# One stage for the three stream branches, with keys laid out by the host

## The reference

```
h = x @ W_in, split into queries, keys, values and gates of three branches
a: causal attention, 8 heads of 64, logit += F[t] - F[s], F = cumsum(log sigmoid(forget gate))
b: window of 128 cached keys (2 key heads for 8 query heads) + own chunk, with a sink per head
c: latent attention: keys and values are projections of a cached latent of 256, + rotary key of 32
branch_n = W_n( attention_n * silu(gate_n) );  m = sum_n sigmoid(g_n) * branch_n
x <- LayerNorm(alpha * x + m @ W_o)
```

## Time and profile before

| | us |
|---|---|
| median of three runs | 3997.64 |
| profiled execution | 3992.19 |
| its span | 3990.5 |
| stream stages of the first layer, a, b, c | 103.0, 43.7, 102.0 |
| stream stages of the second layer | 248.3 |

### The profile page before, as it was taken

One profiled execution on the slowest core, in us unless ns is written; L12 is line 12 of the kernel. 1 busy time (PEld: TensorE's weight loads), 2 busy tenths in 40 slices (PEclk: granted clock), 3 DMA queues, 4 the chain that ended last, 5 costly groups with the idle time before them and its releaser, 6 DMA issues. The chain is left out here.

```text
span 3990.5 us, 57004 instructions
## 1 busy us (share of the span) xinstructions
PE 3496.3 (88%) x21478; PEld 2913.6 (73%) x21478; DVE 1494.3 (37%) x3500; ACT 937.2 (23%) x2080; POOL 122.9 (3%) x64
## 2 busy tenths in 40 slices
PE   1999978998989986789869999789989899758988
PEld 0888856887978864568758888478889788545777
DVE  5114333343333324344531233333333333332546
ACT  1221212332223322220121112123322233212210
POOL 0000000000100000000000000001010000000000
PEclk9999988999999988889979999889999899879999
DMA  5322234223332234353442221433143322433543
GB/s 184 109 94 90 65 116 125 55 65 83 97 85 70 62 93 148 110 192 133 143 152 91 90 88 56 151 87 79 35 109 80 93 61 63 140 125 106 203 148 106
DMA packets 480642, 416.98 MB, mean 104 GB/s; under 512 B 301268, under 2 KB 392020, under 8 KB 478100
## 3 DMA queue, kind: packets, MB, share of 16 engines
q1 hardware_dynamic: 451172, 373.97, 31.1%
q10 hardware_dynamic: 29296, 40.71, 3.0%
HBM read 289.32 MB, written 127.64 MB: 104 GB/s over the span
## 5 line engine op out<-in xcount | busy, mean ns | idle before, releaser
L353 PE MATMUL proj_acc<-proj_wh,keep_xh 128*128 128x512 f32 (+1 forms) x1296 | 502.3, 388 | 12.4 <-DVE proj_wl L328 12.4
L354 PE MATMUL proj_acc<-proj_wl,keep_xh 128*128 128x512 f32 (+1 forms) x1296 | 501.0, 387 | 0.0
L355 PE MATMUL proj_acc<-proj_wh,keep_xl 128*128 128x512 f32 (+1 forms) x1296 | 500.9, 387 | 0.0
L353 PEld LDWEIGHTS proj_acc<-proj_wh,keep_xh 128*128 128x128 f32 x1296 | 244.6, 189 | 58.8 <-DVE proj_wl L328 13.2
L354 PEld LDWEIGHTS proj_acc<-proj_wl,keep_xh 128*128 128x128 f32 x1296 | 244.6, 189 | 45.5
L355 PEld LDWEIGHTS proj_acc<-proj_wh,keep_xl 128*128 128x128 f32 x1296 | 244.5, 189 | 45.5
L1918 PE MATMUL up_acc<-up_wh,up_bh 128*128 128x512 f32 x432 | 173.4, 401 | 12.8 <-DVE up_wl L1962 12.8
L328 DVE TENSOR_TENSOR proj_wl<-proj_raw,proj_wh 128x512 fp32r<-128x512 f32 (+1 forms) x144 | 96.0, 674 | 209.5 <-ACT proj_wh L323 209.5
L1058 PE MATMUL att_b_gacc<-att_b_gwh,keep_xh 128*128 (+1 forms) x576 | 171.0, 297 | 3.6 <-DVE att_b_gwl L1187 3.6
L1058 PE MATMUL att_c_gacc<-att_c_gwh,keep_xh 128*128 (+1 forms) x576 | 170.8, 297 | 3.2 <-DVE att_c_gwl L1187 3.2
L1058 PE MATMUL att_a_gacc<-att_a_gwh,keep_xh 128*128 (+1 forms) x576 | 170.0, 295 | 1.9 <-DVE att_a_gwl L1187 1.9
(11 more groups left out here) (357 smaller groups left out, 7147.1 us busy)
## 6 DMA issues: line engine op xcount, KB each, us to landing
up_gates<-scratch_gates SPq DMA_DIRECT2D x18, 1536.0 KB, 7.6
proj_raw<-in_w_in SPq DMA_DIRECT2D x48, 512.0 KB, 3.7
str_a_kc<-in_cache_a_k SPq DMA_DIRECT2D x16, 1024.0 KB, 5.5
str_a_vc<-in_cache_a_v SPq DMA_DIRECT2D x16, 1024.0 KB, 7.5
scratch_sg<-proj_out SPq DMA_DIRECT2D x54, 256.0 KB, 2.1
up_br<-scratch_br SPq DMA_DIRECT2D x54, 256.0 KB, 8.1
scratch_gates<-att_a_gout SPq DMA_DIRECT2D x24, 384.0 KB, 2.6
scratch_gates<-att_b_gout SPq DMA_DIRECT2D x24, 384.0 KB, 2.7
```

The source lines that it names most:

```text
L353: nc.tensor.matmul(bank, hi, wh[:, u, kt, 0:w], start=kt == 0, stop=False)
L354: nc.tensor.matmul(bank, hi, wl[:, u, kt, 0:w], start=False, stop=False)
L355: mm = nc.tensor.matmul(bank, lo, wh[:, u, kt, 0:w], start=False, stop=kt == KT - 1)
```

## The change

One stage takes the place of the three. Its eight rounds handle streams 0 to 7, each with all three branches, and its loops are written out.

- The host lays out the cached keys of a and b, the rotary keys of c and the key weights of c with positions (or ranks) last. Key tiles of a and b are used as they land, so are c's rotary keys; c's latents are still transposed, since they serve as values too.
- Own columns are 16 per stream: keys are sliced out of one transposed tile, values are loaded per stream to 16 partitions, the own masks of 128 columns are gone. A mask of 16 columns is left for a, in bf16, loaded once at the program's start.
- All streams' query columns are laid out once, in the head; the per-stream copies are gone. The forgetting term is split in a high and a low part in fp32r, so that one pass adds it. b's sink is written to its score column once.
- a and b are not scaled before the turn: the reciprocal and the gate are applied at the copy-out of their values. Their gates are loaded in the layout of the scores, by 8 loads each, issued by ScalarE at the end of its head, and the results are stored by 8 stores each. c is scaled as before.
- Score tiles are single per branch, the probabilities too; the three branches share one output bank, and two transpose banks with fixed readers (ScalarE for one, VectorE for the other).
- SyncE issues a stream's loads in the order keys of a, values of a, c, each behind the wait for its buffer; the early weights come behind the last stream's.

```diff
+        "c_mask_o": neg(np.arange(TS)[None, :] <= qt[:, None]),
...
@@ stream_attention: SyncE @@
+            def load_a(n):
+                u = n % U
+                if n >= U:
+                    sp.wait_ge(sa_made, n - U + 1)
+                sp.dma_start(ka[:, u], T["cache_a_kT"].rearrange("l b (g p) s -> l b p g s", p=P)[l, n])\
+                    .then_inc(a_loaded[u], 16)
+            def load_va(n):
+                u = n % U
+                if n >= U:
+                    sp.wait_ge(pva_made, n - U + 1)
+                sp.dma_start(va[:, u], T["cache_a_v"].rearrange("l b (t p) h d -> l b p t (h d)", p=P)[l, n])\
+                    .then_inc(va_loaded[u], 16)
+                sp.dma_start(voa[:, u], T["s_a_v"].rearrange("l b s h d -> l b s (h d)")[l, n])\
+                    .then_inc(va_loaded[u], 16)
+            def load_c(n):
+                u = n % UC
+                if n >= UC:
+                    sp.wait_ge(pvc_made, n - UC + 1)
+                sp.dma_start(kc[:, u], T["cache_c_kv"].rearrange("l b (t p) r -> l b p t r", p=P)[l, n])\
+                    .then_inc(c_loaded[u], 16)
+                sp.dma_start(pct[:, u], T["cache_c_peT"][l, n]).then_inc(c_loaded[u], 16)
+                sp.dma_start(voc[:, u], T["s_c_kv"][l, n]).then_inc(c_loaded[u], 16)
+            load_a(0)
...
+            for n in range(1, NB):
+                load_a(n)
+                load_va(n)
+                load_c(n)
+            sp.dma_start(C["early"][:], w_br_tiles(T, l)[:, 0:EARLY, :]).then_inc(early_loaded, 16)
+            def place(name, tile, h, wanted):
+                sp.dma_start(S[name][own].rearrange("(n t) (h d) -> h t n d", t=TS, h=H)[h],
+                             tile[h * TS:(h + 1) * TS, :, wanted]).then_inc(stored, 16)
+            sp.wait_ge(oa_taken, NB)
+            for h in range(H):
+                place("br0", oma, h, slice((h % 2) * HD, (h % 2) * HD + HD))
+            sp.wait_ge(ob_taken, NB)
+            for h in range(H):
+                place("br1", omb, h, slice(0, HD))
+            sp.wait_ge(res_ready, 1)
+            sp.dma_start(S["br2"][own], res[:]).then_inc(stored, 16)
+            sp.wait_ge(early_loaded, 16)
+            sp.wait_ge(stored, 16 * (2 * H + 1))
...
@@ TensorE, after the head @@
+            def keys_c(n):
+                u = n % UC
+                pe.wait_ge(c_loaded[u], 48 * (n // UC + 1))
+                for k, (bank, made, taken, group) in enumerate(((tr0, tr0_made, tr0_taken, G0["keys", n]),
+                                                                (tr1, tr1_made, tr1_taken, G1["keys", n]))):
+                    if group > 1:
+                        pe.wait_ge(taken, group - 1)
+                    for j in range(KB):
+                        mm = nc.tensor.transpose(bank[:, j * P:(j + 1) * P], kc[:, u, j, k * P:(k + 1) * P], ident)
+                    mm.then_inc(made, 1)
+            def scores_a(n):
+                u = n % U
+                pe.wait_ge(a_loaded[u], 16 * (n // U + 1))
+                if n >= 1:
+                    pe.wait_ge(exp_a, n)
+                cols = slice(n * TS, (n + 1) * TS)
+                for lo, w, keys in ((0, NK, ka[:, u]), (NK, TS, ktoa[:, :, cols])):
+                    for g in range(4):
+                        nc.tensor.matmul(ssa[32 * g:32 * g + 32, lo:lo + w], qxa[:, n, g, :], keys[:, g, :],
+                                         start=True, stop=False, skip_group_check=True, tile_position=(0, 32 * g))
+                nc.tensor.matmul(ssa[:, 0:NK], selr[:, n, :], fsplit[:, 0:NK], start=False, stop=True,
+                                 skip_group_check=True)
+                nc.tensor.matmul(ssa[:, NK:NK + TS], selr[:, n, :], fsplit[:, NK + n * TS:NK + (n + 1) * TS],
+                                 start=False, stop=False, skip_group_check=True)
+                nc.tensor.matmul(ssa[:, NK:NK + TS], C["ident16"][:], C["mask_o"][:], start=False, stop=True,
+                                 skip_group_check=True).then_inc(sa_made, 1)
+            def scores_b(n):
+                if n == 0:
+                    pe.wait_ge(b_loaded, 48)
+                else:
+                    pe.wait_ge(exp_b, n)
+                nc.tensor.matmul(ssb[:, 0:P], qxb[:, n, :], kb[:, n, :], start=True, stop=True)
+                nc.tensor.matmul(ssb[:, P:P + TS], qxb[:, n, :], ktob[:, n * TS:(n + 1) * TS], start=False, stop=True,
+                                 skip_group_check=True).then_inc(sb_made, 1)
+            def scores_c(n):
+                u = n % UC
+                pe.wait_ge(tr0_taken, G0["keys", n])
+                pe.wait_ge(tr1_taken, G1["keys", n])
+                if n >= 1:
+                    pe.wait_ge(exp_c, n)
+                cols = slice(n * TS, (n + 1) * TS)
+                for lo, w, keys, pes in ((0, NK, ktc[:], pct[:, u]), (NK, TS, ktoc[:, :, cols], kpoc[:, cols])):
                     for k in range(2):
+                        nc.tensor.matmul(ssc[:, lo:lo + w], qac[:, k, n, :], keys[:, k, :], start=k == 0, stop=False)
+                    mm = nc.tensor.matmul(ssc[:, lo:lo + w], qpt[:, n, :], pes, start=False, stop=True)
+                mm.then_inc(sc_made, 1)
...
+            def values_b(n):
+                pe.wait_ge(tr1_taken, G1["b", n])
+                pe.wait_ge(oa_taken, n + 1)
+                for k in range(KVB):
+                    half = slice(k * HD, (k + 1) * HD)
+                    nc.tensor.matmul(oo[half, 0:HD], ptb[:, half], vb[:, n, half], start=True, stop=False,
+                                     skip_group_check=True, tile_position=(0, k * HD))
+                for k in range(KVB):
+                    half = slice(k * HD, (k + 1) * HD)
+                    mm = nc.tensor.matmul(oo[half, 0:HD], pob[:, half], vob[:, n, half], start=False, stop=True,
+                                          skip_group_check=True, tile_position=(0, k * HD))
+                mm.then_inc(pvb_made, 1)
+            def values_c(n):
+                u = n % UC
+                pe.wait_ge(tr0_taken, G0["c", n])
+                pe.wait_ge(tr1_taken, G1["c", n])
+                pe.wait_ge(ob_taken, n + 1)
+                for k in range(2):
+                    for j in range(KB):
+                        nc.tensor.matmul(oo[:, k * P:(k + 1) * P], kc[:, u, j, k * P:(k + 1) * P], ptc[:, j, :],
+                                         start=j == 0, stop=False)
+                    mm = nc.tensor.matmul(oo[:, k * P:(k + 1) * P], voc[:, u, k * P:(k + 1) * P], poc_t[:],
+                                          start=False, stop=True)
+                mm.then_inc(pvc_made, 1)
+            for n in range(NB):
+                keys_c(n)
+                scores_a(n)
+                if n >= 1:
+                    turn_c(n - 1)
+                    values_b(n - 1)
+                scores_b(n)
+                if n >= 1:
+                    values_c(n - 1)
+                turn_a(n)
+                scores_c(n)
+                turn_b(n)
+                values_a(n)
+            turn_c(NB - 1)
+            values_b(NB - 1)
+            values_c(NB - 1)
+            pe.wait_ge(oc_taken, NB)
...
@@ ScalarE, end of its head and the rounds @@
+            for r, sem in ((0, gate_ab), (1, gate_ab)):
                 for h in range(H):
+                    name, tile, cols = (("sg0", sga, slice(h // 2 * P, h // 2 * P + P)),
+                                        ("sg1", sgb, slice(h * HD, (h + 1) * HD)))[r]
+                    const(sem, tile[h * TS:(h + 1) * TS],
+                          S[name][own].rearrange("(n t) c -> t n c", t=TS)[:, :, cols])
+            const(gate_c, sgc[:], S["sg2"][own])
...
+                take(taken, ktc[:, 0, :])
+                if n >= 1:
+                    taken += 1
+                    take(taken, ptc[:].rearrange("p j n -> p (j n)"))
+                exps(ssa, pa, NK + TS, sta, n, max_a, exp_a)
+                exps(ssb, pb, P + TS + 1, stb, n, max_b, exp_b)
+                taken += 1
+                take(taken, pta[:].rearrange("p j n -> p (j n)"))
+                exps(ssc, pc, NK + TS, stc, n, max_c, exp_c)
...
@@ VectorE, the rounds @@
+                nc.vector.tensor_copy(ktc[:, 1, :], tr1[:]).then_inc(tr1_taken, 1)
+                highest(ssa, NK + TS, sta, n, sa_made, max_a)
+                if n >= 1:
+                    taken += 1
+                    take_own(taken, poc_t[:])
+                    if n == 1:
+                        dve.wait_ge(gate_ab, 32 * H)
+                    out_b(n - 1)
+                highest(ssb, P + TS + 1, stb, n, sb_made, max_b)
+                if n >= 1:
+                    out_c(n - 1)
+                taken += 1
+                take_own(taken, poa[:])
+                highest(ssc, NK + TS, stc, n, sc_made, max_c)
+                taken += 1
+                dve.wait_ge(tr1_made, taken)
+                nc.vector.tensor_copy(pob[:], tr1[0:TS, P:2 * P])
```

(57 more changed lines are left out.)

793 lines of the change are left out of this document (271 added, 522 removed).

## The result

The changed kernel takes 3807.9 us (median of 4 runs, 3804.8 to 3809.8) against 3998.9 before: ratio 0.952, 95% interval 0.951 to 0.954. That is 191 us saved where 215 were forecast; the time lies 25 us above the forecast of 3783.

What follows compares the result with a forecast made beforehand. TensorE was taken to bound the rounds, mostly waiting in three heads and tails. Per layer 28.9 + 16 + 82.6 + 13.5 = 141.0 against 248.6 and 248.3, saving 214.9: 3783 us, range 3757 to 3850.

Steps and rivals of the forecast that it cites:

- One stage, one head, one tail; rounds bound by TensorE: Stream stages: one per layer replaces three, 141.0 us against 248.6 and 248.3, TensorE over 95% busy in rounds; chance 0.66.
- hand-offs (14.5): Rival, steady rounds: single banks and tiles stretch a round by 1.28 to 14.5 us, total 3821; chance 0.25.
- half the clock: Rival, all rounds: gaps keep TensorE at 1.2 GHz, +11.3 us a round, total 3961; chance 0.04.
- slow loads: Rival, loads through SyncE in order: under 101 GB/s a round exceeds 27.1 us; at 90 GB/s total 4043; chance 0.02.
- The round, 11.8: Steady round of the merged stage: TensorE's steps plus waits take 11.8 us, bounds 11.1 to 12.6.
- sum of 11.3: TensorE's steps in one round, priced by start-to-start times in the earlier trace, add to 11.3 us before waits.
- 0.4 for b's copy-out: Round: values c waits for values b's copy-out from the shared output bank, 0.4 us, between 0 and 1.0.
- Kept as they are: c's values: Round: c's value passes keep their earlier price, 2 x 1.12 = 2.24 us.
- Own pairs of c at 0.14: Scores of c: three own pairs of 16 columns at 0.14 us each, from a one-column pair, 0.42 together.
- fp32r passes 0.23 apart: Scores of a, forgetting term: one fp32r pass of 512 columns, 0.23 us, replaces a two-pass fp32 matmul of 1.06.
- The first round, 16, behind 17 issues: First round: 17 small gate loads issued by ScalarE take 8.8 us and delay TensorE; 16 us, bounds 9.3 to 21.
- Head 28.9, tail 13.5: Each layer's stage: 28.9 us before the rounds, bounds 24.3 to 43.8, and 13.5 us after them.

Runs made afterwards that it cites:

- pad_pe: Changed kernel with the position part of c's scores (32 rows of weights and keys) zero-filled to 128 rows, own values left at 16 rows: 3800.1 us, ratio 0.950.
- all: Changed kernel with own values of a, b, c and c's position part zero-filled to 128 rows, and gate loads moved off ScalarE's path: 3775.1 us, ratio 0.944.
- best: On top of `all`: scores a ahead of c's key transposes, b's first scores wait for keys alone, second stream's keys loaded before b's values: 3790.3 us, ratio 0.948.
- reorder: Changed kernel with only the order of c's value passes changed, the four 16-row passes together after all 128-row ones: 3798.4 us, ratio 0.950.

## Why the prediction was off by 25 us

- *One stage, one head, one tail; rounds bound by TensorE*: right. TensorE is busy for 13.27 of 13.27 us; the rivals of hand-offs (14.5), of half the clock and of slow loads did not come about. The loads cost nothing in steady rounds, at 207 GB/s.
- *The round, 11.8*: wrong by 1.48, and this is the failed step. Its sum of 11.3 measured 13.27 with hardly a wait (of the 0.4 for b's copy-out about 0.1 is left: scores b's two own passes take 0.30, two such passes of c 0.20 in `pad_pe`). By terms, forecast to measured: values c 2.24 to 2.97, scores c 3.28 to 3.74, scores b 0.36 to 0.62, keys c 0.87 to 1.02, turns 1.30 to 1.58, values a 1.23 to 1.36, values b 0.40 to 0.53, scores a 1.64 to 1.45.
- *"Kept as they are: c's values"*: not kept. The own keys' part shrank from 128 rows to 16, which I did not price. Padding it back took 0.99 off the round: two thirds of the miss.
- *What is left*: with the rows padded in `all` the round is 11.70, still 0.4 above the sum of 11.3. Keys c (1.03 for 0.87), the turns (1.54 for 1.30) and scores b (0.61 for 0.36) are dearer than forecast, the scores of a and c cheaper. The dear ones stand beside tiles of 32 and 64 columns, and there, too, the load does not run ahead: in the changed kernel c's first key transpose behind a's values and its load both start at 1557.10. `best` took one such place out, for 0.11; that the others cost the same was not tried.
- *Own pairs of c at 0.14*: 0.29, the six passes 0.87 where I had 0.42. I took the row of a lone pair between wide passes and set the Trainium skill's 0.21 aside; with equal rows the passes came at 0.10 each (`pad_pe`), and the row changes added 0.28. So 16 columns instead of 128 saved c 0.19 a round, not 0.64.
- *The price stood in the trace before*: in the earlier trace rows c's six own passes take 1.06 where six undisturbed ones would take 0.67; the 32-row pair among them makes most of the difference (0.28 of 0.39 by `pad_pe`). I divided by three and took the quotient for the price of 128 columns.
- *fp32r passes 0.23 apart*: 0.33 here (1545.90 to 1546.23), and no run shows why; still far below the 1.06 of two fp32 passes, and a's scores came out cheaper than forecast.
- *The first round, 16, behind 17 issues*: right in size, 16.8 and 18.6, and in cause for layer one; in layer two 3.4 of the waits were for loads. The issues took 8.96 in place of 8.8. Moved away, they gave back 3.0 and 4.2 of it.
- *Head 28.9, tail 13.5*: within 2.1 us each.

The Trainium skill has the rule that I missed: "TensorEngine Tiling (Array Packing)", Key Properties, says that changing the tiling mode, unlike changing the tile, drains the engine. It does not say that a pass of fewer rows counts as such a change; if it does, `reorder` agrees, with a number: 0.19 us a change between 128 and 16 rows. The Trainium skill's line on weight loads ("TensorE: Matmul & The Clock Gate", LDWEIGHTS), which I rejected, is 107 ns for 128 columns of weights, however few columns move; it agrees as well, with 0.10 a pass of 16 columns in `pad_pe`.

## What to carry to other kernels

On a stretch that TensorE bounds, count the changes of tile shape between neighbouring passes, not only passes and columns: here a part of a few rows was cheaper zero-filled to the rows of its neighbours, or gathered into one block. A busy share of 100% hid this cost; compare the start-to-start time of one group with the same group elsewhere. And a load issue cost its engine half a us here, in order, so put it where that engine waits anyway, and then look what the next stream's loads do.

## What was not expected of the hardware

The same code at the tail ran at either level of the clock. In the changed kernel the 32 closing passes took 3.79 us in layer one and 5.09 in layer two, in `pad_pe` 7.09 in layer one. With the values ahead of them that is some 5 us of one stage. Busy time from the last values of c to the end of those passes, in the changed kernel:

```profile
1612.79:1620.14 7.35, 6.83 (x52) 6.14 (x52) 0.42 (x1) 0.00 (x0) 0.00 (x0) 1.00 0.45 66
```

The same stretch of `pad_pe`:

```profile
1606.24:1618.71 12.47, 11.95 (x52) 10.79 (x52) 0.42 (x1) 0.00 (x0) 0.00 (x0) 0.53 0.26 39
```

The granted clock was 1.00 in the one (2.4 GHz) and about half in the other (1.2 GHz), and 1.00 in the last round of both. What decides between the levels was not tried. It was also not expected that zero-filled rows, which only add multiplications, would make a kernel faster.
